# Four column strips of 344, 344, 172 and 172 instead of three of 344 in the last piece of a down projection and its layer norm

## The chip, the cores and the metric

The kernel runs on one core of a Trainium2 chip, in one launch. The metric is the time of one execution in device microseconds. Lower is better.

## What is computed

One inference step of a decoder layer for 1,024 prompt tokens and 8 sample tokens (1,032 columns in the kernel), with a model width of 1,024 and a feed-forward width of 2,816. Only the last part matters here:

```
h = LN1(alpha * x + Mix(x));   y = LN2(alpha * h + ConvFFN(h))

def _conv_ffn(h, prev, w_up, w_conv, b_conv, w_down):
    up = h @ w_up
    a, gate = up[..., :D_FF], up[..., D_FF:]
    a_c, buf_new = _causal_dwconv(a, w_conv, prev)
    return (jax.nn.gelu(a_c + b_conv) * gate) @ w_down, buf_new

def _layer_norm(x, g, b):
    mu = jnp.mean(xf, axis=-1, keepdims=True)
    var = jnp.mean(jnp.square(xf - mu), axis=-1, keepdims=True)
    return (xf - mu) * lax.rsqrt(var + LN_EPS) * g + b
```

## The kernel before

All activations are held with the channels on the partitions and the 1,032 tokens as columns: `acc` is 128 x 8 x 1032, eight blocks f of 128 output channels. Tokens are cut in thirds of 344 columns (`TW`), `third(j)`. Each fp32 operand is split in a high and a low part of a reduced fp32 type, and a matrix product is made of three: high x high, low weights x high, high weights x low.

The down projection has 22 blocks of the feed-forward width, taken in pieces of 8, 8 and 6 (`PIECES`). The change is in the last piece. For it the weights of all eight output blocks are kept in `wh`/`wl` (f = 0) and `dwh`/`dwl` (f = 1 to 7), so that the loop can run over the columns outside and the output blocks inside: `last_slices` gives (j, f, s), third j, block f, and the slice number s = 8 j + f, from 0 to 23. A slice on TensorE is 6 blocks k x 3 products of 344 columns with a new 128x128 weight for each (L1548), 18 in all, into one of three PSUM banks `U[:, s % 3]`. It waits for `used`, VectorE's count of banks taken, so it can be at most three slices ahead.

VectorE adds the bank to `acc` (L2774, `used`). ScalarE squares the result (`square`, L1861), and VectorE adds it to `total` (which is the buffer `cc`, L2501) and its square to `power` (the buffer `gl`, L2503): `ln_sums`. Which slices' sums follow which add is written in the table `LAST_SUMS`. When the eight blocks of a third are summed, the layer norm of this third goes on:

- `ln_stats` on TensorE: for each 86-column spot (4 of them) a matmul that sums the partitions of `total` and `power` into one column of PSUM (L1372, 86 columns loaded, one moved), and then one of `total` with a matrix of 1/1024 that spreads the mean over all partitions (L1377).
- `ln_moments` on VectorE: three small operations (L2513 to L2515). `root` on GpSimd: the inverse root (L914).
- `ln_spread` on TensorE: four matmuls (L1383) that spread the inverse root over all partitions, 128 columns loaded and 86 moved.
- per pair q of output blocks, `ln_shift` and `ln_scale` on VectorE (L2524, L2530: 688 elements of two blocks), then `affine` on ScalarE (two operations, L1868), then the store of the pair by SyncE (L863).

`LAST_PAIRS` says behind which slice's sums VectorE centres which pair (third, q), `LAST_AFFINE` where ScalarE follows. Statistics and spread of thirds 0 and 1 stand inside TensorE's stream, before block k = 2 of slices 10, 13, 17 and 19. Those of third 2 stand behind the last product, with its four pairs. The matmuls of the layer norm are plain fp32; the trace shows two records for each.

Of the kernel before, what the change touches and what calls it, by code (L numbers as in the profile page):

```python
# [61 lines left out]
SPOTS, SPOT = 4, TW // 4  # L62
PAIRS = KT // 2
# [24 lines left out]
def third(j):  # L88
    return slice(j * TW, (j + 1) * TW)


def build(nc, I, O):
    ctx = ExitStack()
    with ctx:
# [125 lines left out]
        with late:  # L220
            hh = held(late, "hh", [P, KT, TOK], F32R)
            with ExitStack() as zone:
                hf = held(zone, "hf", [P, KT, TOK])
            hl = held(late, "hl", [P, KT, TOK], F32R)
            ab = held(late, "ab", [P, 2 + TOK])
            cc = held(late, "cc", [P, TOK])
            gl = held(late, "gl", [P, TOK])
            fstate = held(late, "fstate", [P, FT, SAMPLES, 2])
            ftails = held(late, "ftails", [P, FT, 10])
            fs_pad = held(late, "fs_pad", [P, 1])  # L230
            lst = held(late, "lst", [P, THIRDS, 12])
# [258 lines left out]
        def last_slices():  # L490

            for j in range(THIRDS):
                for f in range(KT):
                    yield j, f, j * KT + f

        LAST_PAIRS = {13: ((0, 0),), 14: ((0, 1),), 16: ((0, 2), (0, 3)), 19: ((1, 0),), 20: ((1, 1),), 21: ((1, 2),)}
        LAST_AFFINE = {14: ((0, 0),), 15: ((0, 1),), 17: ((0, 2), (0, 3)), 20: ((1, 0),), 21: ((1, 1),), 22: ((1, 2),)}
        LN_CENTRED = (PAIRS, THIRDS * PAIRS + PAIRS)
        LAST_SUMS = {5: (0, 1), 6: (2, 3), 7: (4, 5), 8: (6, 7), 15: (14, 15), 16: (), 22: (21, 22), 23: (23,)}
        SUMMED = {}  # L500
        for s in range(5, 3 * KT):
            for n in LAST_SUMS.get(s, (s - 1,)):
                SUMMED[n] = s
# [4 lines left out]
        LN_BANKS = ((B34[:, 0, :], B34[:, 1, :]), (B56[:, 0, :], B56[:, 1, :]), (B34[:, 0, :], B34[:, 1, :]))  # L508
# [61 lines left out]
        def _(sp):  # L570
# [289 lines left out]
            for j in range(THIRDS):  # L860
                for q in range(PAIRS):
                    sp.wait_ge(ln_aff, (THIRDS + j) * PAIRS + q + 1)
                    sp.dma_start(O["y"][:, two(q), third(j)], acc[:, two(q), third(j)]).then_inc(y_stored, 16)  # L863
            sp.wait_ge(y_stored, 16 * THIRDS * PAIRS)
# [5 lines left out]
        def _(pool):  # L870
# [109 lines left out]
            for j in range(THIRDS):  # L980
                root(1, j)
# [3 lines left out]
        def _(pe):  # L985
# [392 lines left out]

            def ln_spread(ln, j):

                pe.wait_ge(ln_root, ln * THIRDS + j + 1)
                for w in range(SPOTS):
# [155 lines left out]
            for j, f, s in last_slices():  # L1538
                after(pe, used, before + s - 2)
                pe.wait_ge(w_lo, U_LAST + f + 1)  # L1540
                ks = range(PIECES[-1])
                whf, wlf = (wh[:, 0], wl[:, 0]) if f == 0 else (dwh[:, f - 1], dwl[:, f - 1])
                for k in ks:
                    c = slice(k * P, (k + 1) * P)
                    if k == 2 and s in (10, 13, 17, 19):
                        {10: ln_stats, 13: ln_spread, 17: ln_stats, 19: ln_spread}[s](1, s // 16)
# [9 lines left out]
        def _(act):  # L1556
# [300 lines left out]
            def square(f, j, s, count):  # L1857

                act.wait_ge(used, count)
                dst = power[:, third(j)] if f == 0 else ab[:, s % 3 * TW:(s % 3 + 1) * TW]  # L1860
                nc.scalar.activation(dst, acc[:, f, third(j)], ACT.Square).then_inc(ln_sq, 1)  # L1861

            def affine(ln, j, q):

                act.wait_ge(ln_cent, (ln * THIRDS + j) * PAIRS + q + 1)
                for f in (2 * q, 2 * q + 1):
                    g, b = (C_G1, C_B1) if ln == 0 else (C_G2, C_B2)
                    ins = nc.scalar.activation(acc[:, f, third(j)], acc[:, f, third(j)], ACT.Identity,  # L1868
                                               bias=cst[:, b + f:b + f + 1], scale=cst[:, g + f:g + f + 1])
# [20 lines left out]
            for f, j, s in mix_slices():  # L1890
# [4 lines left out]
                square(f, j, s, MIX_USED + s + 1)  # L1895
# [117 lines left out]
            for j, f, s in last_slices():  # L2013
                n = s if f < 4 else max(s, SUMMED[s - 3] + 1)
                square(f, j, s, LAST_USED - 3 * KT + n + 1)
# [8 lines left out]
        def _(dve):  # L2024
# [470 lines left out]
            def ln_sums(f, j, s, count, squares):  # L2495
# [4 lines left out]
                a, t, p = acc[:, f, third(j)], total[:, third(j)], power[:, third(j)]  # L2500
                ls.link(nc.vector.tensor_tensor(t, acc[:, 0, third(j)] if f == 1 else t, a, ALU.add))  # L2501
                dve.wait_ge(ln_sq, squares)
                ins = nc.vector.tensor_tensor(p, p, ab[:, s % 3 * TW:(s % 3 + 1) * TW], ALU.add)  # L2503
# [5 lines left out]
            def ln_moments(ln, j):  # L2509

                dve.wait_ge(ln_stat, ln * THIRDS + j + 1)
                mean, var, scratch = lst[0:SPOT, j, 0:4], lst[0:SPOT, j, 4:8], lst[0:SPOT, j, 8:12]
                ls.link(nc.vector.tensor_copy(lst[0:SPOT, j, 0:8], B7[0:SPOT, 8 * j:8 * j + 8]))  # L2513
# [3 lines left out]
            def spread_of(ln, j, n):  # L2517
                return spread[j][n][:, 0:TW].unsqueeze(1).to_broadcast([P, 2, TW])

            def ln_shift(ln, j, q):  # L2520

                dve.wait_ge(ln_mean, ln * THIRDS + j + 1)
                a = acc[:, two(q), third(j)]
                ls.link(nc.vector.tensor_tensor(a, a, spread_of(ln, j, 0), ALU.subtract))  # L2524

            def ln_scale(ln, j, q):

                dve.wait_ge(ln_wide, ln * THIRDS + j + 1)
                a = acc[:, two(q), third(j)]
# [8 lines left out]
            for f, j, s in mix_slices():  # L2538
# [7 lines left out]
                ln_sums(f, j, s, MIX_USED + s + 1, s + 1)  # L2546
# [222 lines left out]
            for j, f, s in last_slices():  # L2769
                dve.wait_ge(slice_done, 3 * U_LAST + s + 1)  # L2770
                a = acc[:, f, third(j)]
                if s in (10, 17):
                    ln_moments(1, s // 16)
                nc.vector.tensor_tensor(a, a, U[:, s % 3, 0:TW], ALU.add).then_inc(used, 1)  # L2774
                for n in LAST_SUMS.get(s, (s - 1,) if s > 5 else ()):
                    ln_sums(n % KT, n // KT, n, LAST_USED - 3 * KT + n + 1, THIRDS * KT + n + 1)
                for pair in LAST_PAIRS.get(s, ()):
                    ln_centre(1, *pair)
            ln_centre(1, 1, PAIRS - 1)
            ln_moments(1, 2)  # L2780
# [147 lines left out]
```

## Time and profile before

| | |
|---|---|
| median of 3 runs | 1685.33 us |
| lowest and highest of them | 1681.71 and 2676.77 us |
| the profiled execution | 1685.92 us |
| its span, first to last instruction | 1684.1 us |
| mean granted TensorE clock | 0.995 |
| TensorE busy | 98% of the span |
| VectorE, ScalarE, GpSimd busy | 58%, 35%, 31% |

The prediction is made against the profiled execution, whose time is 1.8 us more than its span. The granted clock is a share of 2.4 GHz. A duration of a matmul record reaches over the start of the next, so the distance from start to start is what a matmul costs in a stream; it is called the pitch.

### The profile page before, as it was taken

How to read it: one execution, taken by the hardware profiler on the slowest of the kernel's cores; microseconds unless marked ns; L12 is line 12 of the kernel's file. 1: busy time of each engine (PE TensorE's matmuls, PEld its weight loads, DVE VectorE, ACT ScalarE, POOL GpSimd, SP SyncE). 2: the span in 40 equal slices, each digit the busy share in tenths (PEclk: the TensorE clock that was granted, in tenths of full speed). 3: DMA queues.
4: the chain of work that ended last, by engine and by line, in shares of the span. 5: the costliest groups of instructions: out<-in, count | busy, mean ns of one | idle time of the engine just before them, and what ended most of it. 6: DMA issues, size and time to landing. Idle time of an engine off the chain costs nothing. (4 is left out here: it accounts for less than half of the span.)

```text
span 1684.1 us, 34791 instructions
## 1 busy us (share of the span) xinstructions
PE 1656.2 (98%) x13952; PEld 1601.9 (95%) x13952; DVE 969.8 (58%) x1565; ACT 587.9 (35%) x1190; POOL 526.3 (31%) x287
## 2 busy tenths in 40 slices
PE   8999999999999999999999999999999999999996
PEld 7999999999999888899999999999999999999996
DVE  2001227889466677762853799877777777111157
ACT  3123334444432545542431553222322233201224
POOL 1212111111211112122431424655555554614410
PEclk9999999999999999999999999999999999999998
DMA  4111016445663455426661034444445317431202
GB/s 190 38 50 40 36 37 195 110 122 123 189 212 103 145 158 150 119 90 221 234 235 38 26 139 157 156 156 156 171 168 189 131 75 278 157 117 50 78 8 94
DMA packets 144594, 216.44 MB, mean 129 GB/s; under 512 B 66113, under 2 KB 109409, under 8 KB 142689
## 3 DMA queue, kind: packets, MB, share of 16 engines
q1 hardware_dynamic: 143488, 213.09, 37.7%
q10 hardware_dynamic: 1008, 1.98, 0.4%
q8 instruction: 70, 1.15, 0.3%
q14 instruction: 28, 0.22, 0.0%
HBM read 162.44 MB, written 80.00 MB: 144 GB/s over the span
## 5 line engine op out<-in xcount | busy, mean ns | idle before, releaser
L873 POOL TENSOR_TENSOR wl<-stage,wh 128x1024 fp32r<-128x1024 f32 x81 | 195.7, 2416 | 726.6 <-ACT wh L1565 718.8
L993 PE MATMUL U<-xh,wh 128*128 128x344 f32 x960 | 312.0, 325 | 0.2 <-ACT qkv L1569 0.2
L993 PE MATMUL U<-xl,wh 128*128 128x344 f32 x960 | 307.2, 320 | 0.0
L993 PE MATMUL U<-xh,wl 128*128 128x344 f32 x960 | 307.1, 320 | 0.0
L993 PEld LDWEIGHTS U<-xh,wh 128*128 128x128 f32 x960 | 181.0, 189 | 0.6 <-ACT qkv L1569 0.5
L993 PEld LDWEIGHTS U<-xh,wl 128*128 128x128 f32 x960 | 181.1, 189 | 0.0
L993 PEld LDWEIGHTS U<-xl,wh 128*128 128x128 f32 x960 | 181.0, 188 | 0.0
L1565 ACT ACTIVATE wh<-stage 128x1024 fp32r<-128x1024 f32 x77 | 81.0, 1052 | 131.2 <-PE U L993 108.0
L1104 PE MATMUL U<-xl,wh 128*128 128x344 f32 x384 | 126.3, 329 | 0.0
L1104 PE MATMUL U<-xh,wh 128*128 128x344 f32 x384 | 125.7, 327 | 0.0
L1104 PE MATMUL U<-xh,wl 128*128 128x344 f32 x384 | 125.6, 327 | 0.0
L955 POOL TENSOR_TENSOR wl<-wsum,wh 128x512 fp32r<-128x512 f32 x57 | 90.1, 1594 | 53.2 <-ACT wh L1937 53.2
L2746 DVE SCALAR_TENSOR_TENSOR acc<-acc,U 128x344 f32 (+1 forms) x48 | 24.4, 512 | 139.5 <-PE U L993 138.2
L2567 DVE SCALAR_TENSOR_TENSOR cc<-ab,cst,cc 128x1024 f32<-128x1024 f32 (+2 forms) x52 | 94.0, 1808 | 5.6 <-DVE cc L2565 0.2
L993 PE MATMUL U<-hh,wh 128*128 128x344 f32 x280 | 90.0, 322 | 1.9 <-DVE cc L2591 1.1
L1480 PE MATMUL B<-hh,qh 128*128 128x258 f32 x320 | 90.7, 283 | 0.4 <-DVE ab L2656 0.4
L1480 PE MATMUL B<-xh,wh 128*128 128x258 f32 x320 | 90.4, 282 | 0.0
L1480 PE MATMUL B<-hh,ql 128*128 128x258 f32 x320 | 90.3, 282 | 0.0
L1480 PE MATMUL B<-hl,qh 128*128 128x258 f32 x320 | 90.3, 282 | 0.0
L1480 PE MATMUL B<-xh,wl 128*128 128x258 f32 x320 | 90.2, 282 | 0.0
L1480 PE MATMUL B<-xl,wh 128*128 128x258 f32 x320 | 90.0, 281 | 0.0
L993 PE MATMUL U<-hl,wh 128*128 128x344 f32 x280 | 89.3, 319 | 0.0
(456 smaller groups left out, 4441.8 us busy)
## 6 DMA issues: line engine op xcount, KB each, us to landing
stage<-in_wu SPq DMA_DIRECT2D x126, 512.0 KB, 4.3
out_shift<-in_cache SPq DMA_DIRECT2D x16, 1022.0 KB
hid_scr<-cc SPq DMA_DIRECT2D x22, 516.0 KB, 3.0
gate_scr<-gth SPq DMA_DIRECT2D x16, 516.0 KB, 3.5
gates<-gate_scr SPq DMA_DIRECT2D x8, 1032.0 KB, 5.9
dn_scr<-thb SPq DMA_DIRECT2D x12, 512.0 KB, 2.9
tok_scr<-pre SPq DMA_DIRECT2D x48, 128.0 KB, 4.0
qkv<-in_cache SPq DMA_DIRECT2D x10, 512.0 KB, 6.7
```

The source lines that it names most:

```text
L873: nc.gpsimd.tensor_tensor(wl[:, par, :], stage[:, par, :], wh[:, par, :].bitcast(F32), ALU.subtract).then_inc(w_lo, 1)
L955: nc.gpsimd.tensor_tensor(l, SOURCE[p][0], fp(h), ALU.subtract).then_inc(q_low.sem, 1)
L993: ins = nc.tensor.matmul(dst, a[:, par, w], b[:, xk, third(j)], start=first and n == 0 and m == 0, stop=last and n == len(ks) - 1 and m == 2)
L1104: ins = nc.tensor.matmul(U[:, j, 0:TW], a[:, par, k * P:(k + 1) * P], x[:, k, third(j)], start=m == 0, stop=m == 3 * KT - 1)
L1480: ins = nc.tensor.matmul(bank[:, q, :], a[:, c], x[:, k, t], start=k == 0 and m == 0, stop=k == KH - 1 and m == 2)
L1565: nc.scalar.activation(wh[:, par, :], stage[:, par, :], ACT.Copy).then_inc(w_hi, 1)
L2567: st.link(nc.vector.scalar_tensor_tensor(cc[:, a:a + w], ab[:, a + k:a + k + w], w3[k], cc[:, a:a + w], ALU.mult, ALU.add))
L2746: nc.vector.scalar_tensor_tensor(a, a, scale, U[:, j, 0:TW], ALU.mult, ALU.add).then_inc(used, 1)
```

## The change

The last piece and the second layer norm get four strips: the first two are the thirds 0 and 1, and third 2 is cut in two strips of 172 columns. The slices go from 24 to 32, and the last 16 have products of 172 columns. `spots` and `strip` give a strip's count of 86-column spots (4 or 2) and its columns. Every operation of the layer norm takes its widths from them. The first layer norm keeps its thirds. The tables of the slices are written anew. Strips use the banks B34, B56, B34, B56 for mean and root.

```diff
+STRIPS = THIRDS + 1
+def spots(ln, j):
+    return SPOTS if ln == 0 or j < 2 else SPOTS // 2
+
+def strip(ln, j):
+    a = third(j).start if ln == 0 or j < 2 else (j + 2) * TW // 2
+    return slice(a, a + spots(ln, j) * SPOT)
...
-            for j in range(THIRDS):
+            for j in range(STRIPS):
                 for f in range(KT):
                     yield j, f, j * KT + f
...
+        LAST_STATS, LAST_SPREAD = {10: 0, 18: 1, 26: 2}, {12: 0, 20: 1, 28: 2}
+        LN_CENTRED = {(0, 2): PAIRS, (1, 2): (THIRDS + 1) * PAIRS, (1, 3): (THIRDS + 2) * PAIRS}
...
-            for j in range(THIRDS):
+            for j in range(STRIPS):
                 for q in range(PAIRS):
                     sp.wait_ge(ln_aff, (THIRDS + j) * PAIRS + q + 1)
-                    sp.dma_start(O["y"][:, two(q), third(j)], acc[:, two(q), third(j)]).then_inc(y_stored, 16)
+                    sp.dma_start(O["y"][:, two(q), strip(1, j)], acc[:, two(q), strip(1, j)]).then_inc(y_stored, 16)
...
-                    for w in range(SPOTS):
-                        a, c = j * TW + w * SPOT, 8 * j + n * SPOTS + w
+                    for w in range(spots(ln, j)):
+                        a, c = strip(ln, j).start + w * SPOT, 8 * j + n * spots(ln, j) + w
...
-                if j == 2:
-                    pe.wait_ge(ln_cent, LN_CENTRED[ln])
-                nc.tensor.matmul(spread[j][0][:, 0:TW], inv[:], total[:, third(j)], start=True, stop=True).then_inc(ln_mean, 1)
+                if j >= 2:
+                    pe.wait_ge(ln_cent, LN_CENTRED[ln, j])
+                nc.tensor.matmul(spread[j][0][:, 0:spots(ln, j) * SPOT], inv[:], total[:, strip(ln, j)], start=True,
+                                 stop=True).then_inc(ln_mean, 1)
...
-                        ins = nc.tensor.matmul(U[:, s % 3, 0:TW], a[:, c], b[:, k, third(j)], start=k == 0 and m == 0,
-                                               stop=k == ks[-1] and m == 2)
+                        ins = nc.tensor.matmul(U[:, s % 3, 0:spots(1, j) * SPOT], a[:, c], b[:, k, strip(1, j)],
+                                               start=k == 0 and m == 0, stop=k == ks[-1] and m == 2)
                 ins.then_inc(slice_done, 1)
-            ln_stats(1, 2)
-            ln_spread(1, 2)
+            ln_stats(1, STRIPS - 1)
+            ln_spread(1, STRIPS - 1)
...
-            affine(1, 1, PAIRS - 1)
+            affine(1, 2, PAIRS - 1)
             for q in range(PAIRS):
-                affine(1, 2, q)
+                affine(1, 3, q)
...
-                nc.vector.tensor_tensor(a, a, U[:, s % 3, 0:TW], ALU.add).then_inc(used, 1)
+                nc.vector.tensor_tensor(a, a, U[:, s % 3, 0:spots(1, j) * SPOT], ALU.add).then_inc(used, 1)
```

The end of TensorE's queue, before: the last three products and the layer norm of third 2.

```order
L1548 MATMUL U<-xh,dwh 128x344
L1548 MATMUL U<-xh,dwl 128x344
L1548 MATMUL U<-xl,dwh 128x344
L1372 MATMUL B7<-cst,cc 86x1 x4
L1372 MATMUL B7<-cst,gl 86x1 x4
L1377 MATMUL B34<-cc,inv 128x344
L1383 MATMUL B34<-cst,lst 128x86 x4
```

The same place with the change, for strip 3.

```order
L1564 MATMUL U<-xh,dwh 128x172
L1564 MATMUL U<-xh,dwl 128x172
L1564 MATMUL U<-xl,dwh 128x172
L1385 MATMUL B7<-cst,cc 86x1 x2
L1385 MATMUL B7<-cst,gl 86x1 x2
L1390 MATMUL B56<-cc,inv 128x172
L1397 MATMUL B56<-cst,lst 128x86 x2
```

The products are as many in a slice and half as wide, and half of the layer norm's matmuls remain here; the other half, strip 2's, now stands in the stream, at slices 26 and 28.

The end of VectorE's queue, before, from the sums of slice 23: `cc` and `gl` are the two sums, L2524 and L2530 the shift and the scale of a pair.

```order
L2501 TENSOR_TENSOR cc<-cc,acc 128x344
L2503 TENSOR_TENSOR gl<-gl,ab 128x344
L2524 TENSOR_TENSOR acc<-acc,B56 128x2x344
L2530 TENSOR_TENSOR acc<-acc,B56 128x2x344
L2513 COPY lst<-B7 86x8
L2514 TENSOR_TENSOR lst<-lst 86x4
L2515 SCALAR_TENSOR_TENSOR lst<-lst 86x4
L2524 TENSOR_TENSOR acc<-acc,B34 128x2x344 x4
L2530 TENSOR_TENSOR acc<-acc,B34 128x2x344 x4
```

The same place with the change, from the add of slice 31 and the sums of slices 30 and 31.

```order
L2793 TENSOR_TENSOR acc<-acc,U 128x172
L2518 TENSOR_TENSOR cc<-cc,acc 128x172
L2520 TENSOR_TENSOR gl<-gl,ab 128x172
L2518 TENSOR_TENSOR cc<-cc,acc 128x172
L2520 TENSOR_TENSOR gl<-gl,ab 128x172
L2543 TENSOR_TENSOR acc<-acc,B34 128x2x172
L2549 TENSOR_TENSOR acc<-acc,B34 128x2x172
L2531 COPY lst<-B7 86x4
L2532 TENSOR_TENSOR lst<-lst 86x2
L2533 SCALAR_TENSOR_TENSOR lst<-lst 86x2
L2543 TENSOR_TENSOR acc<-acc,B56 128x2x172 x4
L2549 TENSOR_TENSOR acc<-acc,B56 128x2x172 x4
```

The order of the steps is the same, each at half its width; one pair of the strip before still stands ahead of the moments.

## Rows read from the trace of the kernel before

**Rows 1.** The page, part 1: busy us (share of the span) and count, by engine

```profile
PE 1656.2 (98%) x13952; PEld 1601.9 (95%) x13952; DVE 969.8 (58%) x1565; ACT 587.9 (35%) x1190; POOL 526.3 (31%) x287
```

**Rows 2.** Chain that ended last, from 1510 us: start, us, what

```profile
1621.71 1.15 PE B L1372 x16
1622.87 0.69 PE B L1377 x2
...
1632.06 0.86 PE B L1383 x8
...
1668.63 2.05 PE B L1372 x16
1670.68 1.37 PE B L1377 x2
...
1672.08 0.88 DVE acc L2524
```

**Rows 3.** Timeline of VectorE: start, us, operation, [idle before and releaser]

```profile
1598.21 0.51 DVE L2774 TENSOR_TENSOR acc<-acc,U 128x344 f32<-128x344 f32 x1 [2.22 <-PE U L1548]
1601.03 0.52 DVE L2774 TENSOR_TENSOR acc<-acc,U 128x344 f32<-128x344 f32 x1 [2.31 <-PE U L1548]
...
1643.88 0.50 DVE L2774 TENSOR_TENSOR acc<-acc,U 128x344 f32<-128x344 f32 x1
...
1661.09 0.51 DVE L2774 TENSOR_TENSOR acc<-acc,U 128x344 f32<-128x344 f32 x1
1661.52 0.51 DVE L2501 TENSOR_TENSOR cc<-cc,acc 128x344 f32<-128x344 f32 x1
...
1662.61 0.87 DVE L2524 TENSOR_TENSOR acc<-acc,B 128x688 f32<-128x688 f32 x1
...
1664.31 0.50 DVE L2774 TENSOR_TENSOR acc<-acc,U 128x344 f32<-128x344 f32 x1
...
1670.72 0.16 DVE L2513 COPY lst<-B 86x8 f32<-86x8 f32 x1 [0.45 <-PE B L1372]
```

**Rows 4.** Timeline of TensorE, and L1377's durations in ns (least, median, most)

```profile
1622.73 0.82 PE L1377 MATMUL B<-cc,inv 128*128 128x344 f32 x2
...
1665.55 0.31 PE L1548 MATMUL U<-xl,dwh 128*128 128x344 f32 x1
...
1672.40 2.01 PE L1383 MATMUL B<-cst,lst 86*128 86x86 f32 x8 [0.36 <-POOL lst L914]
...
L1377 PE MATMUL B<-cc,inv x12: 452/536/922, 919.9 to 1671.3; 128*128 128x344 f32 x12
```

**Rows 5.** Stretches: us, busy by engine (count), granted clock, DMA share, GB/s

```profile
530.00:720.00 190.00, 187.16 (x3139) 165.23 (x3137) 136.13 (x339) 94.84 (x262) 32.57 (x22) 1.00 0.49 143
1669.40:1672.20 2.80, 2.64 (x11) 1.62 (x11) 1.46 (x5) 1.24 (x2) 0.86 (x1) 0.50 0.00 0
```

**Rows 6.** Timeline of TensorE: first and last of 28 products of 258 columns

```profile
1299.76 0.28 PE L1480 MATMUL U<-xl,wh 128*128 128x258 f32 x1
...
1302.96 0.28 PE L1480 MATMUL B<-xl,wh 128*128 128x258 f32 x1
```

**Rows 7.** Weight loads by line: least, median and most ns of a load

```profile
L1383 PEld LDWEIGHTS B<-cst,lst x48: 187/190/333, 930.4 to 1673.8; 86*128 86x128 f32 x48
...
L1281 PEld LDWEIGHTS B<-XTq,Y x1024: 101/108/108, 539.5 to 735.5; 32*32 32x32 f32 x171
```

**Rows 8.** Groups by form: busy us, mean ns of one, idle before

```profile
L2358 DVE TENSOR_TENSOR Lb<-LTq,dcst 128x128 f32<-128x128 f32 x24 | 6.9, 288 | 0.4
L1621 ACT ACTIVATE pb<-sb,stat 128x128 f32<-128x128 f32 x52 | 20.4, 394 | 10.6 <-DVE stat L2117 10.6
L1621 ACT ACTIVATE pb<-sb,stat 128x256 f32<-128x256 f32 x44 | 22.0, 500 | 21.4 <-DVE stat L2117 21.4
```

**Rows 9.** Timeline of ScalarE (last eight affines); time to landing of y's stores

```profile
1676.60 4.64 ACT L1868 ACTIVATE acc<-acc,cst 128x344 f32<-128x344 f32 x8 [5.06 <-DVE acc L2530]
...
DMA to landing us min/median/max: 2.4/2.4/3.0
```

More of the change, by code:

```diff
@@ L230, in build @@
             fs_pad = held(late, "fs_pad", [P, 1])
-            lst = held(late, "lst", [P, THIRDS, 12])
+            lst = held(late, "lst", [P, STRIPS, 12])
             inv = held(late, "inv", [P, P])
@@ L490, in last_slices @@
         def last_slices():
-            for j in range(THIRDS):
+            for j in range(STRIPS):
                 for f in range(KT):
                     yield j, f, j * KT + f
[L496 to L499, printed above, removed]
+        LAST_PAIRS = {12: ((0, 0),), 13: ((0, 1),), 14: ((0, 2),), 16: ((0, 3),), 20: ((1, 0),), 22: ((1, 1),), 24: ((1, 2),),
+                      27: ((1, 3),), 28: ((2, 0),), 29: ((2, 1),), 30: ((2, 2),)}
+        LAST_AFFINE = {s + 1: pairs for s, pairs in LAST_PAIRS.items()}
+        LAST_STATS, LAST_SPREAD = {10: 0, 18: 1, 26: 2}, {12: 0, 20: 1, 28: 2}
+        LN_CENTRED = {(0, 2): PAIRS, (1, 2): (THIRDS + 1) * PAIRS, (1, 3): (THIRDS + 2) * PAIRS}
+        LAST_SUMS = {5: (0, 1), 6: (2, 3), 7: (4, 5), 8: (6, 7), 15: (14, 15), 16: (), 23: (22, 23), 24: (), 31: (30, 31)}
         SUMMED = {}
-        for s in range(5, 3 * KT):
+        for s in range(5, STRIPS * KT):
             for n in LAST_SUMS.get(s, (s - 1,)):
@@ L506, in two @@
             return slice(2 * q, 2 * q + 2)
-        LN_BANKS = ((B34[:, 0, :], B34[:, 1, :]), (B56[:, 0, :], B56[:, 1, :]), (B34[:, 0, :], B34[:, 1, :]))
+        LN_BANKS = ((B34[:, 0, :], B34[:, 1, :]), (B56[:, 0, :], B56[:, 1, :])) * 2
         OPEN_A, OPEN_B = (U[:, 0, 0:TW], U[:, 2, 0:TW], U[:, 0, 0:TW]), (U[:, 1, 0:TW], B7[:, 0:TW], U[:, 2, 0:TW])
@@ L859, in _ @@
             sp.dma_start(O["ffnconv"], ftails[:]).then_inc(ftail_stored, 16)
-            for j in range(THIRDS):
+            for j in range(STRIPS):
                 for q in range(PAIRS):
                     sp.wait_ge(ln_aff, (THIRDS + j) * PAIRS + q + 1)
-                    sp.dma_start(O["y"][:, two(q), third(j)], acc[:, two(q), third(j)]).then_inc(y_stored, 16)
-            sp.wait_ge(y_stored, 16 * THIRDS * PAIRS)
+                    sp.dma_start(O["y"][:, two(q), strip(1, j)], acc[:, two(q), strip(1, j)]).then_inc(y_stored, 16)
+            sp.wait_ge(y_stored, 16 * STRIPS * PAIRS)
             sp.wait_ge(ftail_stored, 16)
@@ L913, in root @@
                 pool.wait_ge(ln_var, ln * THIRDS + j + 1)
-                nc.gpsimd.tensor_tensor(lst[0:SPOT, j, 8:12], lst[0:SPOT, j, 4:8], mhalf[0:SPOT, 0:SPOTS], ALU.pow).then_inc(
+                n = spots(ln, j)
+                nc.gpsimd.tensor_tensor(lst[0:SPOT, j, 8:8 + n], lst[0:SPOT, j, n:2 * n], mhalf[0:SPOT, 0:n], ALU.pow).then_inc(
                     ln_root, 1)
@@ L979, in _ @@
                 nc.gpsimd.tensor_tensor(dwl[:, n, :], src, dwh[:, n, :].bitcast(F32), ALU.subtract).then_inc(w_lo, 1)
-            for j in range(THIRDS):
+            for j in range(STRIPS):
                 root(1, j)
@@ L1374, in ln_stats @@
                 ins.then_inc(ln_stat, 1)
-                if j == 2:
-                    pe.wait_ge(ln_cent, LN_CENTRED[ln])
-                nc.tensor.matmul(spread[j][0][:, 0:TW], inv[:], total[:, third(j)], start=True, stop=True).then_inc(ln_mean, 1)
+                if j >= 2:
+                    pe.wait_ge(ln_cent, LN_CENTRED[ln, j])
+                nc.tensor.matmul(spread[j][0][:, 0:spots(ln, j) * SPOT], inv[:], total[:, strip(ln, j)], start=True,
+                                 stop=True).then_inc(ln_mean, 1)
             def ln_spread(ln, j):
                 pe.wait_ge(ln_root, ln * THIRDS + j + 1)
-                for w in range(SPOTS):
+                for w in range(spots(ln, j)):
                     ins = nc.tensor.matmul(spread[j][1][:, w * SPOT:(w + 1) * SPOT],
@@ L1544, in _ @@
                     c = slice(k * P, (k + 1) * P)
-                    if k == 2 and s in (10, 13, 17, 19):
-                        {10: ln_stats, 13: ln_spread, 17: ln_stats, 19: ln_spread}[s](1, s // 16)
+                    if k == 2 and s in LAST_STATS:
+                        ln_stats(1, LAST_STATS[s])
+                    if k == 2 and s in LAST_SPREAD:
+                        ln_spread(1, LAST_SPREAD[s])
                     for m, (a, b) in enumerate(((whf, xh), (wlf, xh), (whf, xl))):
-                        ins = nc.tensor.matmul(U[:, s % 3, 0:TW], a[:, c], b[:, k, third(j)], start=k == 0 and m == 0,
-                                               stop=k == ks[-1] and m == 2)
+                        ins = nc.tensor.matmul(U[:, s % 3, 0:spots(1, j) * SPOT], a[:, c], b[:, k, strip(1, j)],
+                                               start=k == 0 and m == 0, stop=k == ks[-1] and m == 2)
                 ins.then_inc(slice_done, 1)
-            ln_stats(1, 2)
-            ln_spread(1, 2)
+            ln_stats(1, STRIPS - 1)
+            ln_spread(1, STRIPS - 1)
         @block.scalar
@@ L1856, in _, with square @@
                 merge_high(f)
-            def square(f, j, s, count):
+            def square(ln, f, j, s, count):
                 act.wait_ge(used, count)
-                dst = power[:, third(j)] if f == 0 else ab[:, s % 3 * TW:(s % 3 + 1) * TW]
-                nc.scalar.activation(dst, acc[:, f, third(j)], ACT.Square).then_inc(ln_sq, 1)
+                dst = power[:, strip(ln, j)] if f == 0 else ab[:, s % 3 * TW:s % 3 * TW + spots(ln, j) * SPOT]
+                nc.scalar.activation(dst, acc[:, f, strip(ln, j)], ACT.Square).then_inc(ln_sq, 1)
             def affine(ln, j, q):
@@ L1867, in affine @@
                     g, b = (C_G1, C_B1) if ln == 0 else (C_G2, C_B2)
-                    ins = nc.scalar.activation(acc[:, f, third(j)], acc[:, f, third(j)], ACT.Identity,
+                    ins = nc.scalar.activation(acc[:, f, strip(ln, j)], acc[:, f, strip(ln, j)], ACT.Identity,
                                                bias=cst[:, b + f:b + f + 1], scale=cst[:, g + f:g + f + 1])
@@ L1894, in _ @@
                     ffn_high(s - 17)
-                square(f, j, s, MIX_USED + s + 1)
+                square(0, f, j, s, MIX_USED + s + 1)
                 for pair in MIX_AFFINE.get(s, ()):
@@ L2014, in _ @@
                 n = s if f < 4 else max(s, SUMMED[s - 3] + 1)
-                square(f, j, s, LAST_USED - 3 * KT + n + 1)
+                square(1, f, j, s, LAST_USED - 3 * KT + n + 1)
                 for pair in LAST_AFFINE.get(s, ()):
                     affine(1, *pair)
-            affine(1, 1, PAIRS - 1)
+            affine(1, 2, PAIRS - 1)
             for q in range(PAIRS):
-                affine(1, 2, q)
+                affine(1, 3, q)
         @block.vector
@@ L2493, in _, with ln_sums @@
             spread = LN_BANKS
-            def ln_sums(f, j, s, count, squares):
+            def ln_sums(ln, f, j, s, count, squares):
                 if f == 0:
@@ L2499, in ln_sums @@
                 dve.wait_ge(used, count)
-                a, t, p = acc[:, f, third(j)], total[:, third(j)], power[:, third(j)]
-                ls.link(nc.vector.tensor_tensor(t, acc[:, 0, third(j)] if f == 1 else t, a, ALU.add))
+                c = strip(ln, j)
+                a, t, p = acc[:, f, c], total[:, c], power[:, c]
+                ls.link(nc.vector.tensor_tensor(t, acc[:, 0, c] if f == 1 else t, a, ALU.add))
                 dve.wait_ge(ln_sq, squares)
-                ins = nc.vector.tensor_tensor(p, p, ab[:, s % 3 * TW:(s % 3 + 1) * TW], ALU.add)
+                ins = nc.vector.tensor_tensor(p, p, ab[:, s % 3 * TW:s % 3 * TW + spots(ln, j) * SPOT], ALU.add)
                 if f == KT - 1:
@@ L2511, in ln_moments @@
                 dve.wait_ge(ln_stat, ln * THIRDS + j + 1)
-                mean, var, scratch = lst[0:SPOT, j, 0:4], lst[0:SPOT, j, 4:8], lst[0:SPOT, j, 8:12]
-                ls.link(nc.vector.tensor_copy(lst[0:SPOT, j, 0:8], B7[0:SPOT, 8 * j:8 * j + 8]))
+                n = spots(ln, j)
+                mean, var, scratch = lst[0:SPOT, j, 0:n], lst[0:SPOT, j, n:2 * n], lst[0:SPOT, j, 8:8 + n]
+                ls.link(nc.vector.tensor_copy(lst[0:SPOT, j, 0:2 * n], B7[0:SPOT, 8 * j:8 * j + 2 * n]))
                 ls.link(nc.vector.tensor_tensor(scratch, mean, mean, ALU.mult))
@@ L2517, in spread_of @@
             def spread_of(ln, j, n):
-                return spread[j][n][:, 0:TW].unsqueeze(1).to_broadcast([P, 2, TW])
+                w = spots(ln, j) * SPOT
+                return spread[j][n][:, 0:w].unsqueeze(1).to_broadcast([P, 2, w])
             def ln_shift(ln, j, q):
                 dve.wait_ge(ln_mean, ln * THIRDS + j + 1)
-                a = acc[:, two(q), third(j)]
+                a = acc[:, two(q), strip(ln, j)]
                 ls.link(nc.vector.tensor_tensor(a, a, spread_of(ln, j, 0), ALU.subtract))
@@ L2528, in ln_scale @@
                 dve.wait_ge(ln_wide, ln * THIRDS + j + 1)
-                a = acc[:, two(q), third(j)]
+                a = acc[:, two(q), strip(ln, j)]
                 nc.vector.tensor_tensor(a, a, spread_of(ln, j, 1), ALU.mult).then_inc(ln_cent, 1)
@@ L2545, in _ @@
                 nc.vector.scalar_tensor_tensor(a, a, ALPHA, U[:, s % 3, 0:TW], ALU.mult, ALU.add).then_inc(used, 1)
-                ln_sums(f, j, s, MIX_USED + s + 1, s + 1)
+                ln_sums(0, f, j, s, MIX_USED + s + 1, s + 1)
                 for pair in MIX_PAIRS.get(s, ()):
@@ L2770, in _ @@
                 dve.wait_ge(slice_done, 3 * U_LAST + s + 1)
-                a = acc[:, f, third(j)]
-                if s in (10, 17):
-                    ln_moments(1, s // 16)
-                nc.vector.tensor_tensor(a, a, U[:, s % 3, 0:TW], ALU.add).then_inc(used, 1)
+                a = acc[:, f, strip(1, j)]
+                if s in LAST_STATS:
+                    ln_moments(1, LAST_STATS[s])
+                nc.vector.tensor_tensor(a, a, U[:, s % 3, 0:spots(1, j) * SPOT], ALU.add).then_inc(used, 1)
                 for n in LAST_SUMS.get(s, (s - 1,) if s > 5 else ()):
-                    ln_sums(n % KT, n // KT, n, LAST_USED - 3 * KT + n + 1, THIRDS * KT + n + 1)
+                    ln_sums(1, n % KT, n // KT, n, LAST_USED - 3 * KT + n + 1, THIRDS * KT + n + 1)
                 for pair in LAST_PAIRS.get(s, ()):
                     ln_centre(1, *pair)
-            ln_centre(1, 1, PAIRS - 1)
-            ln_moments(1, 2)
+            ln_centre(1, 2, PAIRS - 1)
+            ln_moments(1, 3)
             for q in range(PAIRS):
-                ln_shift(1, 2, q)
+                ln_shift(1, 3, q)
             for q in range(PAIRS):
-                ln_scale(1, 2, q)
+                ln_scale(1, 3, q)
 def layout(x):
```

## The prediction

> **What bounds the kernel now.** I read the page's busy shares first: TensorE is busy 98% of the span and VectorE 58% [rows 1], so far down the program the time is TensorE's queue of products. The chain that ended last says where this stops. It runs on TensorE's products without a gap through thirds 0 and 1 and into third 2, the layer norm's matmuls of L1372, L1377 and L1383 standing in the stream; in third 2 it changes to VectorE, and goes on by TensorE's last layer-norm matmuls, VectorE and ScalarE to the end [rows 2, 9]. So there are two regimes here, and I price them apart: up to the last product, TensorE's stream; behind it, a tail in which the last strip is normalised.
>
> The last product starts at 1665.55 [rows 4]; with one product's pitch it is through at 1665.71. The tail is the other 18.4 us up to 1684.1. Its marks: VectorE still owes two slices of sums and the add of slice 23, TensorE starts the statistics at 1668.63, VectorE starts the moments at 1670.72 and the four subtractions of the mean at 1672.08, ScalarE starts its eight affine operations at 1676.60 and ends at 1681.24, and the last store lands [rows 2, 3, 9]. The clock row matters too: TensorE stands idle from 1665.71 to 1668.63, and the granted clock is then 0.50 of 2.4 GHz, that is 1.2 GHz, from 1669.4 on [rows 5].
>
> **Part 1, the products of the narrow strips.** The change replaces 8 slices x 18 products of 344 columns by 16 x 18 products of 172. The columns are the same; the weight loads are twice as many, one 128x128 load ahead of each product, as now. What a slice costs now: VectorE's adds of slices 1 and 2 start 2.82 us apart [rows 3], so a product has a pitch of 0.1567 us, which is 344 columns at 2.4 GHz (0.1433) and 13 ns. Eight slices are 22.56 us.
>
> No row has such a product at 172 columns, so the pitch is bounded from both sides. Going on by width alone: at 258 columns 27 steps take 3.20 us, a pitch of 0.1185 [rows 6]; the line through 258 and 344 gives 0.080 at 172. Against this stand the loads. A load's record takes 190 ns at 128 columns and 108 at 32 [rows 7]: 0.85 ns a column on a fixed part of some 80 ns, so 109 ns of it go with the 128 columns. That this sets a pitch is seen in the layer norm's own matmuls. The sixteen of L1372 load 86 columns and move one; they take 1.15 us, 72 ns each, 0.84 ns a loaded column. The eight of L1383 load 128 columns and take 0.86 us, 107.5 ns each [rows 2], though they move only 86 columns; by the L1377 rows, where the second of two matmuls of 344 columns starts 0.82 - 0.54 = 0.28 us behind the first [rows 4], moving 86 takes 72 ns, precisely what 172 columns of the products would take. So the nearest row in what is loaded and in what is moved is L1383, and I take 0.1075 us. The upper bound is the pitch at 258, 0.119, if the stream of products never steps faster than that.
>
> The Trainium skill, "TensorE: Matmul & The Clock Gate", section "LDWEIGHTS (loading the stationary operand)", gives a load as its columns divided by 1.2 in ns, so 107 ns, and that speaks against this change. The rows on L1372 and L1383 agree with it; with it as the only limit this part is +8.3. The same page's section "Back-to-back issue gap" gives a stream of load and product about 81 ns at 128 columns and 131 at 512; an estimate on the line between them is 87 ns at 172, which would make this part +2.5; L1383 doesn't bear it out.
>
> At 0.1075, 288 products take 30.96 us: **+8.40 us**. At 0.119: +11.7.
>
> **Part 2, one more strip's layer norm within the stream.** Before, two strips' statistics and spreads stand in the stream and the third's in the tail. Now three stand in it: strip 2's is half a strip, so half of 1.15 (statistics), of 0.69 (mean) and of 0.86 (spread) [rows 2]: **+1.35 us**. TensorE thus ends at 1665.71 + 9.75 = 1675.46, provided that nobody holds it up. The waits that are added in its queue have all other products behind them: the sums at slices 18 and 26, the roots at 20 and 28. Strip 1's statistics come at slice 18 now, some 4.5 us into strip 2 where it was 3.8 at slice 17, and there they had no gap before them [rows 2]; strip 2's have the same two slices of distance. The mean of strip 3 waits for the pairs of strip 1, the last of which is centred at slice 27. GpSimd has one more root, ScalarE eight more squares, SyncE four more stores; all of it lies beside the stream, since ScalarE is busy 35% and GpSimd 31% [rows 1].
>
> **Part 3, does VectorE keep up?** A dependent step costs its duration and some 30 ns, an independent one some 90 ns less than its duration [rows 3]: an add 0.43, two sums 1.09 or 0.55 each, a shift and a scale 1.70 together, 0.90 and 0.79. In third 2 of before, a slice with a pair comes to 3.2 us against TensorE's 2.82 (slices 21 and 22 are 3.22 apart, [rows 3]); that is the backlog that stands at the end. Narrow steps: 344 and 688 elements take 0.51 and 0.87 us [rows 3], and 128 elements 0.288 [rows 8], so 172 elements are 0.33 and each step is 0.18 shorter. A narrow slice is 0.25 + 2 x 0.37 = 0.99 us, with a narrow pair 0.99 + 0.54 + 0.43 = 1.96, with a pair of strip 1 0.99 + 1.69 = 2.7. TensorE's slice is 18 x 0.1075 = 1.94. The pairs of strip 1 stand at every second slice (20, 22, 24, then 27), so VectorE catches up between; the narrow pairs at 28 to 30 run at TensorE's pace. VectorE is not the bound, and comes some 0.6 us late to slice 31.
>
> **Part 4, the tail.** Counted from the last product. Start of the statistics: 0.6, the add 0.25, and the four sums of slices 30 and 31 at 0.37: 2.3 us, where it was 2.92. The statistics are 8 matmuls for 16, 0.58 us with the clock still up, but VectorE has pair (2, 3) to centre meanwhile (0.97), so the moments start at 3.3 us, where it was 5.01: 1.7 less. Moments to first shift: it was 1.36, because the mean's matmul took 1.37 at the low clock; now the mean is there when the moments are done, 0.47: 0.9 less. Four shifts and the first scale: 4.52 before, now 4 x 0.54 + 0.53 = 2.7: 1.8 less. Eight affines: 0.58 each before (4.64 for eight, [rows 9]). From 128 to 256 elements a ScalarE operation grows from 394 to 500 ns [rows 8], so 0.83 ns an element, 0.14 less at 172: 3.5 us, 1.15 less. The store: 2.4 us to landing now [rows 9], half the bytes, between nothing and 0.45 us less; I take 0.2. Together the tail is 12.6 us for 18.4: **-5.8 us**. The four smaller spread matmuls hide under the shifts at either clock. If TensorE's idle 2.3 us are enough for the clock to fall before the statistics, 0.5 us of the gain are lost.
>
> **The sum.** 8.40 + 1.35 - 5.8 = +3.95 us on a span of 1684.1, so 1688.05. The profiled execution took 1685.92, 1.8 more than its span and 0.6 above the median of 1685.33; with it **1689.9 us, say 1690**, 0.3% slower than before. The gain in the tail is real, and costs more than it brings, because half-width products don't take half the time. Bounds: at a pitch of 0.119 the sum is +7.3 (1693.2); with the low clock and no gain in the store another 0.7.
>
> **Rivals.** *Loads hidden, chance 0.14.* The products step at 0.080. The stream is then only 0.6 + 1.35 us longer, but VectorE becomes the bound: from slice 16 on it has 16 x 0.99, five wide pairs at 1.69, three narrow at 0.97 and two moments of 0.4, 28 us from 1643.88 [rows 3], so its sums end no earlier than 1671.9 and with its idle gaps about 1672.7, 3.3 to 4 later than the 1668.6 of before; behind that point it has 0.97 + 0.47 + 2.7 + 3.5 + 2.65 = 10.3 us, or up to 0.7 more with the clock down, for 15.5. Net -1.9 to -0.4: 1684 to 1685.5, faster than my forecast and at most a shade faster than before. For it: the slope from 344 to 258. Against it: L1383. The Trainium skill's 87 ns ("TensorE: Matmul & The Clock Gate", section "Back-to-back issue gap") would end at about the same time, since VectorE is then still the bound.
>
> *The one-pass mode is lost at narrow widths, chance 0.10; this is the case on the other side.* The products take one pass of one cycle a column at 344 and at 258; nothing in the trace shows that they do at less. Plain matmuls here show two records of two cycles a column (L1377, [rows 4]). If the narrow products fell to that, each would take 4 x 172 / 2.4 = 0.287 us, 288 of them 82.6 for 22.56: +60.0, +1.35, -5.8, so 1741.5 us, 3.3% slower. It decides from a pitch of 0.21, where the sum passes 2%. Against it: the instruction and its types are unchanged.
>
> *Half clock, chance 0.04.* While loads set the pace the array moves columns 72 ns of every 107. If the clock then fell to 1.2 GHz, the pitch is that of L1383 in the tail, (2.01 - 0.51)/7 = 0.214 us [rows 4]: 61.6 for 22.56, net +34.6, 1720.5, just over 2%. Against it: the clock reads 1.00 throughout 530 to 720, where the products are mixed with 32-column matmuls [rows 5].
>
> **Chances.** My case (pitch 0.107 to 0.119) has 0.68; 0.04 is for what I don't see. The likeliest case by itself spans 1689 to 1694. The range of 1683 to 1696 takes in that and the hidden loads, 0.8 together. About 2% is what a measurement of this kernel can tell from no change: faster by over 2% 0.02, within 2% 0.84, slower 0.14 (the lost mode and the half clock).
>
> **What would show it.** In the profile after: 288 product records at 172 columns stepping by 0.107 to 0.119 us; last product near 1675.5; statistics some 2.3 us behind it; VectorE idle between the adds of strip 2 and 3 in slices without pairs; ScalarE's last eight affines in 3.5 us; 12.6 us from last product to end. The pitch alone makes or breaks the number: each 10 ns in it is 2.9 us.

## The result, and the profile after

The changed kernel takes 1690.38 us (median of 6 runs, 1689.17 to 1693.74); the kernel before, on the same chip, 1684.13 us. The ratio is 1.0037, 95% interval [1.0026, 1.0048]: 0.4% slower, clear of the noise and within 2%. One of the six executions of the kernel before took 2676.77 us and counts in its median; the median of the other five is 1683.68. The forecast was 1690, 0.3% slower. The profiled execution took 1690.73 us, its span is 1688.9 us, 4.8 us more than before.

The last part of the chain that ended last, of the changed kernel (start, us, what):

```profile
1630.18 15.09 PE U L1564 x108
1645.27 1.15 PE B L1385 x16
...
1651.98 12.06 PE U L1564 x108
1664.05 0.54 PE B L1385 x8
1664.59 0.40 PE B L1390 x2
...
1678.71 0.81 PE B L1385 x8
1679.52 0.80 PE B L1390 x2
```

L1564 are the products, L1385 the statistics, L1390 the mean. The piece from 1651.98 on is all narrow: 108 products of 172 columns in 12.06 us, 0.1117 us each. At the pitch of the wide ones in [rows 3] as many would take 16.9 us, so half the columns save 29%, not half. The rows at 1664.05 and 1664.59 are the third layer norm that the stream now holds, 0.54 and 0.40 us where a whole third takes 1.15 and 0.69 in [rows 2].

The timeline of TensorE near the end gives the pitch from two products 42 steps apart; the second is the last product:

```profile
1671.83 0.27 PE L1564 MATMUL U<-xl,dwh 128*128 128x172 f32 x1
...
1676.51 0.27 PE L1564 MATMUL U<-xl,dwh 128*128 128x172 f32 x1
```

4.68 / 42 = 0.1114 us. The last product is through at 1676.62, where it was 1665.71. Behind it, the timelines of VectorE and ScalarE:

```profile
1673.66 0.34 DVE L2520 TENSOR_TENSOR gl<-gl,ab 128x172 f32<-128x172 f32 x1
1674.03 0.51 DVE L2543 TENSOR_TENSOR acc<-acc,B 128x344 f32<-128x344 f32 x1
...
1676.96 0.33 DVE L2793 TENSOR_TENSOR acc<-acc,U 128x172 f32<-128x172 f32 x1
...
1679.55 0.16 DVE L2531 COPY lst<-B 86x4 f32<-86x4 f32 x1
...
1680.34 2.15 DVE L2543 TENSOR_TENSOR acc<-acc,B 128x344 f32<-128x344 f32 x4 [0.24 <-PE B L1390]
...
1683.07 3.48 ACT L1884 ACTIVATE acc<-acc,cst 128x172 f32<-128x172 f32 x8 [2.47 <-DVE acc L2549]
```

Four shifts take 2.15 us and eight affines 3.48; ScalarE's eight were 4.64 in [rows 9]. VectorE's last add starts only 0.34 us behind the last product. The tail is 12.3 us for 18.4. The clock, by stretches (start and end, length, busy us with counts for TensorE, its weight loads, VectorE, ScalarE and GpSimd, granted clock, DMA share, GB/s):

```profile
1640.00:1675.00 35.00, 35.00 (x318) 34.80 (x318) 26.01 (x64) 13.69 (x31) 1.70 (x2) 1.00 0.20 72
1677.50:1678.70 1.20, 0.00 (x0) 0.00 (x0) 1.09 (x5) 1.01 (x3) 0.00 (x0) 1.00 0.47 143
1677.50:1680.00 2.50, 1.29 (x10) 1.15 (x10) 2.29 (x9) 1.36 (x4) 0.00 (x0) 0.86 0.45 133
1680.00:1682.00 2.00, 1.38 (x6) 0.93 (x4) 1.65 (x5) 0.61 (x2) 0.69 (x1) 0.50 0.27 83
```

It is 1.00 through all the narrow products, and still while TensorE waits for the last sums; it falls while the statistics run, which start at 1678.71. In the kernel before it was the same: 1.00 through the wait, and 0.50 from 1669.4 on [rows 5], when the statistics had begun at 1668.63.

```profile
1665.70:1668.60 2.90, 0.16 (x2) 0.00 (x0) 2.69 (x7) 1.27 (x3) 0.00 (x0) 1.00 0.34 123
```

### The profile page after: what moved, and what is told of

Its sections match the earlier page's. It is cut to its first block and busy times, and to the rows that moved or that the text cites. A ratio compares the mean times of both kernels' runs of the same rounds, so it can differ in the third digit from the quotient of the medians.

```text
span 1688.9 us, 35163 instructions
## 1 busy us (share of the span) xinstructions
PE 1664.8 (99%) x14098; PEld 1611.2 (95%) x14098; DVE 972.9 (58%) x1598; ACT 590.3 (35%) x1206; POOL 526.2 (31%) x288
```

## Experiments

Seven kernels, made from the changed one except where the heading says otherwise. The kernel before was timed beside them on the same chip: 1685.00 us for experiments 1, 2, 4 and 5, 1685.08 us on another chip for the others. Ratios are to it. The changed kernel was not timed again on these chips.

**1. Is it the load? Half the load under the same product (one execution).**

```diff
+                        rows = P if j < 2 else P // 2
-                        ins = nc.tensor.matmul(U[:, s % 3, 0:spots(1, j) * SPOT], a[:, c], b[:, k, strip(1, j)],
-                                               start=k == 0 and m == 0, stop=k == ks[-1] and m == 2)
+                        ins = nc.tensor.matmul(U[0:rows, s % 3, 0:spots(1, j) * SPOT], a[:, k * P:k * P + rows],
+                                               b[:, k, strip(1, j)], start=k == 0 and m == 0, stop=k == ks[-1] and m == 2)
```

> The changed kernel (strips of 344, 344, 172, 172), with the products of the two narrow strips loading 64 of the 128 output channels; the other half of the output in these columns is left out, so the time stands for less work. Theory 1, the weight load sets the pitch of narrow products: 64 columns load in half the time, the pitch falls from 0.111 us to what 172 columns need, 0.080 to 0.088; TensorE then runs ahead of VectorE, VectorE sets the end of the stream, and the span falls from 1688.9 to about 1684 to 1685. Theory 2, a matmul has a floor of some 0.11 us whatever it loads: pitch 0.111 and span 1689 as now.

Measured: 1685.72 us, span 1683.9. Timeline of TensorE, two products 25 steps apart, and the chain behind the stream:

```profile
1649.87 0.24 PE L1565 MATMUL U<-xh,dwl 128*64 128x172 f32 x1
...
1651.87 0.25 PE L1565 MATMUL U<-xl,dwh 128*64 128x172 f32 x1
```

```profile
1655.30 0.35 DVE gl L2521
1655.67 0.88 DVE acc L2544
...
1673.16 1.33 PE B L1385 x8
1674.49 0.80 PE B L1390 x2
```

2.00 / 25 = 0.080 us. The columns moved, their number and the waits are those of the changed kernel; only the columns loaded are halved (and with them the output channels written), and the pitch falls from 0.111 to 0.080. Theory 1 holds, theory 2 falls. The span is 5.0 us shorter, though 288 x 0.031 = 8.9 us went out of the products: the chain now runs over VectorE's sums and shifts through much of strips 2 and 3, and the statistics start at 1673.16, 4.4 us behind the last product. So even with the loads made cheap the four strips are only level with the kernel before (1685.0), as far as one execution tells.

**2. The same question by width: strips of 344, 344, 258, 86 (4 executions).**

```diff
-STRIPS = THIRDS + 1
+SPLIT = (4, 4, 3, 1)
+STRIPS = len(SPLIT)
...
 def spots(ln, j):
-    return SPOTS if ln == 0 or j < 2 else SPOTS // 2
+    return SPOTS if ln == 0 else SPLIT[j]
...
 def strip(ln, j):
-    a = third(j).start if ln == 0 or j < 2 else (j + 2) * TW // 2
+    a = third(j).start if ln == 0 else sum(SPLIT[:j]) * SPOT
```

> Strips of 344, 344, 258 and 86 columns. Theory 1, the load sets the pitch below about 258 columns: the 86-column products have a pitch of 0.107 to 0.111 us like those of 172, the 258-column ones 0.1185 as elsewhere in the kernel; the stream is 33 us for the last two strips for 32.1 in the changed kernel, the tail is 1 us shorter, and the time is that of the changed kernel within 1 us, 1690. Rival, the pitch goes with the width plus a constant (0.040 from 172 columns on): 86 columns take 0.075 us, the stream is 5 us shorter and VectorE holds it: 1686 to 1687.

Measured: 1701.93 us, ratio 1.0100 [1.0085, 1.0116], 12 us above what theory 1 gave and more above the rival. The timeline of TensorE in the last strip, and the stretches:

```profile
1660.92 0.29 PE L1565 MATMUL U<-xl,wh 128*128 128x86 f32 x1
...
1664.94 0.39 PE L1565 MATMUL U<-xl,dwh 128*128 128x86 f32 x1
...
1679.48 0.42 PE L1565 MATMUL U<-xh,dwl 128*128 128x86 f32 x1
...
1691.00 0.42 PE L1565 MATMUL U<-xh,dwl 128*128 128x86 f32 x1
```

```profile
1660.00:1665.00 5.00, 5.00 (x47) 5.00 (x45) 4.79 (x11) 1.83 (x4) 0.00 (x0) 1.00 0.27 92
1665.00:1670.00 5.00, 5.00 (x28) 4.81 (x26) 0.96 (x2) 1.40 (x3) 0.00 (x0) 0.50 0.34 126
...
1680.00:1685.00 5.00, 5.00 (x25) 5.00 (x25) 2.98 (x9) 2.14 (x6) 0.00 (x0) 0.50 0.19 70
```

At the full clock 36 steps take 4.02 us: 0.1117 us at 86 columns, the same as at 172. That is theory 1's answer; the pitch doesn't depend on the width from 172 columns down. But at 1665 the granted clock goes to 0.50, to 1.2 GHz, with TensorE busy 5.00 us of every 5.00 ahead of it and behind it, and stays there: 54 steps in 11.52 us, 0.213 each. The mean granted clock was 0.988 to 0.990 in all four executions, where it is 0.994 to 0.997 in the six of the changed kernel, so it wasn't a single case. Neither theory had this. It is the mechanism of the prediction's rival "half clock", which didn't come at 172 columns and comes at 86.

**3. What took the clock? The same loads, twice the columns (one execution, from experiment 2).**

```diff
+                        cols = strip(1, j) if j < 3 else slice(TOK - 2 * SPOT, TOK)
-                        ins = nc.tensor.matmul(U[:, s % 3, 0:spots(1, j) * SPOT], a[:, c], b[:, k, strip(1, j)],
+                        ins = nc.tensor.matmul(U[:, s % 3, 0:cols.stop - cols.start], a[:, c], b[:, k, cols],
...
+                off = 0 if j < 3 else SPOT
-                nc.vector.tensor_tensor(a, a, U[:, s % 3, 0:spots(1, j) * SPOT], ALU.add).then_inc(used, 1)
+                nc.vector.tensor_tensor(a, a, U[:, s % 3, off:off + spots(1, j) * SPOT], ALU.add).then_inc(used, 1)
```

> Strips of 344, 344, 258, 86, where each product of the last strip moves the 172 last columns for its 86 (the 86 before them too, into a part of the bank that nobody reads). The loads, their number and their pitch stay. In the kernel with 86 columns moved the granted clock went to 0.50 in the middle of this strip, at 1665, with TensorE never idle. Theory A, it fell because so few columns are moved beside each load: with 172 moved the clock stays at 1.00 to the last product, the pitch is 0.111 us in the whole strip, and the span is 1688 to 1691, as the changed kernel's. Theory B, a stream held by its loads loses the clock by itself, whatever it moves: the clock falls again and the span is near 1701.

Measured: 1689.65 us, span 1687.8. The stretches in the last strip, and two of its products 30 steps apart:

```profile
1665.00:1670.00 5.00, 5.00 (x45) 4.95 (x44) 1.96 (x10) 1.55 (x4) 0.94 (x1) 1.00 0.19 72
1670.00:1675.00 5.00, 5.00 (x48) 5.00 (x46) 4.68 (x11) 2.46 (x6) 0.00 (x0) 1.00 0.16 58
```

```profile
1668.19 0.27 PE L1566 MATMUL U<-xh,dwl 128*128 128x172 f32 x1
...
1671.54 0.28 PE L1566 MATMUL U<-xh,dwl 128*128 128x172 f32 x1
```

The pitch is 3.35 / 30 = 0.1117 us, and the clock stays at 1.00 up to the last product. Twice the columns moved cost nothing, and the kernel is 12 us faster by it (1689.65 for 1701.93; the two ran on different chips, on which the kernel before takes the same within 0.1 us). Theory A holds: with the same loads at the same pitch, what differs is the columns moved beside them. Where between 86 and 172 columns the clock is lost, no run here shows.

**4. Is it the fourth strip or its width? Four strips of 258 (11 executions).** `SPLIT = (3, 3, 3, 3)` in the diff of experiment 2.

> Four equal strips of 258 columns, with the tables of the changed kernel. Theory 1: 576 products at 0.1185 us take 68.3 us against 67.7 for the 432 of 344 columns, so four strips cost TensorE only 0.6 us of products and 1.4 of layer norm, VectorE's narrower tail gives 2 to 3 back, VectorE's backlog takes some of it: 1684 to 1686, that is 4 to 6 below the changed kernel and within 2 us of the kernel before. Rival, what costs is the fourth strip itself (its 8 more slices, waits and layer norm steps) and not the loads: 1689 to 1691.

Measured: 1687.01 us, ratio 1.0012 [1.0003, 1.0021]. Two thirds of the change's loss are gone, with the same 32 slices, waits and four layer norms; the rival's 1689 to 1691 is not met. But it is 1 us above the range, and not faster than before. The chain of waits shows why:

```profile
1661.34 0.04 DVE acc L2794
1661.38 0.30 issue
1661.68 0.43 DVE cc L2519
...
1671.31 1.92 PE B L1386 x12
1673.23 1.08 PE B L1391 x2
```

It leaves TensorE's stream at 1661.3. The last product is through at 1667.57, only 1.9 us later than before, as worked out; VectorE's sums end 3.7 us behind it (2.9 before), since a slice with a pair takes it 2.58 us for TensorE's 2.13, and the clock is down again when the statistics run (1.92 us for the 12 of a strip; 0.85 in the stream). The tail is 17.1 us for 18.4, where I had counted on 2 to 3 us less.

**5. What the low clock costs in the tail (11 executions, from the kernel before).**

```diff
+            pe.wait_ge(used, LAST_USED - 2)
+            for n in range(18):
+                nc.tensor.matmul(U[:, 0, 0:TW], whf[:, c], xh[:, k, third(2)], start=True, stop=True)
             ln_stats(1, 2)
```

> The kernel before, with 18 more products of 344 columns behind TensorE's last slice into a PSUM bank that nobody reads any more, so that TensorE is not idle for the 2.9 us in which it waits for the last sums. Theory: the statistics and the mean of the last third run at 2.4 GHz then (1.15 and 0.69 us for 2.05 and 1.37), VectorE's wait of 0.45 and 0.81 us for them shrinks, and the time is 1.0 to 1.5 us lower than that of the kernel before. Rival, the low clock is not what VectorE waits for there (the latency of the chain is): less than 0.3 us.

Measured: 1683.60 us against 1685.00, ratio 0.9991 [0.9982, 1.0000]: 1.4 us less, the size that was forecast, but the interval reaches 1.0000, so the time alone doesn't exclude the rival. The stretch of the statistics and the timelines of TensorE and VectorE show it better:

```profile
1667.40:1668.50 1.10, 1.10 (x16) 1.10 (x15) 1.07 (x2) 0.00 (x0) 0.00 (x0) 1.00 0.00 0
```

```profile
1664.47 2.96 PE L1553 MATMUL U<-xh,dwh 128*128 128x344 f32 x18
1667.40 0.77 PE L1372 MATMUL B<-cst,cc 128*86 128x1 f32 x8
...
1669.51 3.59 DVE L2527 TENSOR_TENSOR acc<-acc,B 128x688 f32<-128x688 f32 x4
```

The clock is 1.00 while the statistics run, and the first shift starts 5.04 us behind the last real product, where it was 6.37 [rows 2, 4]: 1.3 us less, with no wait of VectorE for the mean.

**6 and 7. GpSimd adds up the outputs (12 executions each).** Both from the changed kernel: three strips of 344 with the tables of before and 9 filler products, and four of 258 with 8.

```diff
+            for j, f, s in last_slices():
...
+                nc.gpsimd.tensor_tensor(total[:, c], acc[:, 0, c] if f == 1 else total[:, c], acc[:, f, c],
+                                        ALU.add).then_inc(total_sum, 1)
...
-                ls.link(nc.vector.tensor_tensor(t, acc[:, 0, c] if f == 1 else t, a, ALU.add))
+                if ln == 0:
+                    ls.link(nc.vector.tensor_tensor(t, acc[:, 0, c] if f == 1 else t, a, ALU.add))
```

> Three strips of 344 as in the kernel before, but GpSimd, idle there, adds the outputs of a strip up (the sum; VectorE keeps the sum of squares), and 9 products of 344 columns that nobody reads keep TensorE busy behind the last slice. VectorE has 0.55 us less in each slice and 1.1 less behind the last one. Theory, VectorE's backlog and the low clock are 2.5 to 3 us of the old tail: 1681 to 1683 where the kernel before takes 1684 to 1685. Rival, GpSimd's addition (about 1 us for 344 columns from its other rows) or its use of SBUF beside VectorE slows VectorE by as much as it takes over: 1684 to 1687.

Measured: 1682.57 us against 1685.08, ratio 0.9985 [0.9977, 0.9994], inside the forecast range.

> Four strips of 258 columns with the same two edits (GpSimd adds up, 8 products of 258 columns as filler). Loads cost nothing at this width, VectorE no longer falls behind in slices with a pair (2.1 us for TensorE's 2.13), and the tail is that of a strip of 258: stream +2.0, tail -5.4 against the kernel before, so 1681 to 1682, 3 to 4 us below the kernel before and about 9 below the changed one. Rival as above, GpSimd slows VectorE: 1685 to 1687, no better than four strips of 258 without it.

Measured: 1684.03 us, ratio 0.9993 [0.9985, 1.0002], 2 us above the range: level with the kernel before, and 3 us better than four strips of 258 without the two edits. In its profiled execution, of 1682.81 us, the last product is through at 1667.11 and the tail is 13.9 us, 4.5 less than before where I had counted on 5.4; the rest of the miss is between this execution and the median. Timelines of TensorE, GpSimd and VectorE in experiment 6:

```profile
1664.44 1.56 PE L1583 MATMUL U<-xh,dwh 128*128 128x344 f32 x9
1666.65 0.77 PE L1399 MATMUL B<-cst,cc 128*86 128x1 f32 x8 [0.65 <-DVE gl L2539]
```

```profile
1659.58 1.15 POOL L1004 TENSOR_TENSOR cc<-cc,acc 128x344 f32<-128x344 f32 x1 [1.70 <-DVE acc L2812]
1662.41 1.13 POOL L1004 TENSOR_TENSOR cc<-cc,acc 128x344 f32<-128x344 f32 x1 [1.68 <-DVE acc L2812]
1665.30 0.92 POOL L1004 TENSOR_TENSOR cc<-cc,acc 128x344 f32<-128x344 f32 x1 [1.77 <-DVE acc L2812]
```

```profile
1659.42 0.51 DVE L2539 TENSOR_TENSOR gl<-gl,ab 128x344 f32<-128x344 f32 x1
1659.96 0.87 DVE L2562 TENSOR_TENSOR acc<-acc,B 128x688 f32<-128x688 f32 x1
...
1662.98 0.93 DVE L2539 TENSOR_TENSOR gl<-gl,ab 128x344 f32<-128x344 f32 x1 [0.23 <-ACT ab L1895]
...
1665.85 0.75 DVE L2539 TENSOR_TENSOR gl<-gl,ab 128x344 f32<-128x344 f32 x1 [0.63 <-ACT ab L1895]
...
1668.76 3.58 DVE L2562 TENSOR_TENSOR acc<-acc,B 128x688 f32<-128x688 f32 x4
```

The filler's first product starts at 1664.44, so there the last real product is through; the first shift follows 4.32 us later, 5.04 with the filler alone (experiment 5), 6.37 before. An addition takes GpSimd 0.92 to 1.15 us. VectorE's sum of squares takes 0.51 us where it starts ahead of GpSimd's addition (1659.42); the one at 1662.98 starts inside an addition that ends at 1663.54, and takes 0.93, until 0.37 us behind that end. The last one, at 1665.85, takes 0.75. So the rival is partly right: some 0.2 us of the gain are lost in the tail, where the two come together. Experiment 6 is the fastest kernel here, 2.5 us (0.15%) below the one before. The filler alone gave 1.4 us in experiment 5, but the intervals of the two ratios overlap, so GpSimd's part rests on the 0.7 us between 5.04 and 4.32, from one trace each.

## Why the prediction was right

**Part 1, the pitch.** I took 0.1075 us from the layer norm's matmuls, with 0.119 as the upper end; it is 0.1114. 288 products cost 32.1 us for 22.56, +9.5 where the sum had +8.4. The mechanism is shown by experiments 1 and 2: half the load brings the pitch to 0.080, half the columns leave it at 0.112. The value sits 4 ns above L1383's; where these 4 ns come from, no run shows. The Trainium skill, "TensorE: Matmul & The Clock Gate", section "LDWEIGHTS (loading the stationary operand)", gives 107 ns for the load; the trace agrees within these 4 ns. The same page's "Back-to-back issue gap", by which I had an estimate of 87 ns, doesn't hold for these products: 111 measured.

**Part 2, the third layer norm in the stream.** +1.35 worked out. TensorE's end moved by 10.9 us in all, so 1.4 beside the products; 0.94 of it are the statistics and the mean at 1664.05 and 1664.59.

**Part 3, VectorE.** Not the bound, as said. It is 0.34 us late at the last add, 0.6 worked out.

**Part 4, the tail.** From the last product: statistics at 2.1 us (2.3 worked out), moments at 2.9 (3.3), first shift at 3.7 (3.8), affines at 6.5 (6.5), their end at 9.9 (10.0), the end at 12.3 (12.6). The clock did fall before the statistics were through (0.81 us for 0.54 in the stream), and the first shift waited 0.24 us for the mean; this was named as a possible loss of 0.5. It was made up by the earlier start of the statistics. The store of 172 KB lands faster by more than I took, 0.5 us for 0.2. Sum: -6.1 for -5.8.

So +10.9 and -6.1 give +4.8 where the text had +9.75 and -5.8. The two misses partly cancel. The one term off by more than a half us is the pitch. That the median came out within 0.4 us of the forecast is in part luck: the profiled execution, by which the sum was made, lies 0.8 us above it, and the medians are 6.25 us apart, where the traces have 4.8 and the forecast had 4. Executions of the same kernel differ by up to 4.6 us here (1689.17 to 1693.74), so a miss of that size says nothing about the sum.

**Rivals.** *Loads hidden*: not the case, but experiment 1 makes it so, and gives 1685.72 where 1684 to 1685.5 was worked out (for less work), with VectorE as the bound and the statistics at 1673.2 (1672.7 worked out). *The one-pass mode lost*: no; the products move one column a cycle at 172, since the step of 80 ns in experiment 1 has room for 172 columns once (72 ns), not for more passes. *Half clock*: not at 172 columns; at 86 it is real and costs 12 us there. I had given it 0.04 for 172 columns and priced its pitch at 0.214; experiment 2 measured 0.213.

## What to carry to other kernels

Cutting a tile in two along the moved columns shortens a tail, but every weight tile is then loaded twice: work out the pitch as the larger of load and columns before the cut, from a row that loads as many columns and moves few, and keep the width near the point where both are equal: 258 columns are 107.5 ns at 2.4 GHz, as much as the load of 128 takes in [rows 2], and their pitch is 0.1185 [rows 6]. Compare what the cut costs in the stream (here 10.9 us) with what it gives in the tail (6.1), and look for cheaper means on the tail first: keeping TensorE busy while it waits, and an idle engine for one of two sums, brought 2.5 us together. Don't let a long stretch move few columns beside full loads without reading its granted clock.

## What was not expected of the hardware

- TensorE lost its clock (1.00 to 0.50 at 1665, experiment 2) while its queue was never empty: it took a 128x128 load and a product of 86 columns every 0.112 us. With 172 columns at the same pitch it kept 1.00 for all of the last strips, both in the changed kernel and in experiment 3. Moving more columns than needed made the kernel 12 us faster. Each is one traced execution.
- Without the load as its limit, a product of 172 columns steps by 0.080 us, 8 ns above its columns; at 344 it is 13 ns (0.1567).
- VectorE and GpSimd slow each other by form: `gl<-gl,ab`, with both inputs in SBUF, took 0.93 us for 0.51 when it started inside a GpSimd addition, while the shift at 1659.96, with one input in PSUM, took its usual 0.87 inside one. The other way round, GpSimd's additions took 1.13 and 1.15 us where VectorE's sum of squares had started just ahead, and 0.92 at 1665.30, where it had not. The Trainium skill, "GPSIMD Engine Reference", section "1. Specifications", says that the two contend when VectorE's instruction has two SBUF inputs; these rows agree.
